# A mixer block and an attention block on one core: HGRN operands built earlier, S5 outputs asked for every six gate units, and the split-off gate units recounted

## The reference

```python
h = rms_norm(x, mix_norm)
(u_a, q_b, f_b, i_b, og_b, cx_c, v_c, o_c, ig_c, fg_c, gates) = split(h @ w_in)
y_a = s5_mixer(u_a, ...)       # complex diagonal state space, 32 groups x 64 states
y_b = hgrn2_mixer(q_b, f_b, i_b, og_b, ...)   # gated linear attention, 6 heads of 128
y_c = mlstm_mixer(cx_c, v_c, o_c, ig_c, fg_c, ...)
merged = (sigmoid(g_a) * (y_a @ wb_a) + sigmoid(g_b) * (y_b @ wb_b) + sigmoid(g_c) * (y_c @ wb_c))
x = x + merged @ w_out
x = x + conv_ffn(rms_norm(x, ffn_norm), ...)
```

## Time and profile before

| | |
|---|---|
| median of three runs | 3015.6 us |
| the profiled execution, its time | 3018.68 us |
| its span in the profile | 3016.9 us |
| PE busy | 2962.8 us (98%) |
| DVE busy | 2051.3 us (68%) |
| ACT busy | 1311.4 us (43%) |
| mean granted clock of TensorE | 0.994 |

### The profile page before, as it was taken

One profiled execution on the slowest core, in us unless ns is written; L12 is line 12 of the kernel. 1 busy time (PEld: TensorE's weight loads), 2 busy tenths in 40 slices (PEclk: granted clock), 3 DMA queues, 4 the chain that ended last, 5 costly groups with the idle time before them and its releaser, 6 DMA issues.

```text
span 3016.9 us, 47095 instructions
## 1 busy us (share of the span) xinstructions
PE 2962.8 (98%) x18616; PEld 2640.7 (88%) x18616; DVE 2051.3 (68%) x2624; ACT 1311.4 (43%) x1418; POOL 70.3 (2%) x72
## 2 busy tenths in 40 slices
PE   8999999889999999999999999999999999999999
PEld 8898898889988888888888888886998888888888
DVE  6674787866778888885557776636667666666444
ACT  5354424334444444444444344425444444444333
POOL 0000000000001000000000000000000000000000
PEclk9999999999999999999999999999999999999999
DMA  6553334445555555555555554531455555555555
GB/s 227 182 188 131 119 112 141 140 134 202 183 193 195 195 193 191 190 184 184 187 188 200 194 182 167 182 136 56 168 181 195 191 190 191 194 194 179 193 194 186
DMA packets 87359, 530.39 MB, mean 176 GB/s; under 512 B 9952, under 2 KB 10336, under 8 KB 41184
## 3 DMA queue, kind: packets, MB, share of 16 engines
q1 hardware_dynamic: 87264, 529.07, 50.4%
HBM read 526.94 MB, written 2.10 MB: 175 GB/s over the span
## 4 chain that ended last, share of the span: by engine, by line
PE 94%; DVE 4%; ACT 1%; issue 0%; DMA 0%; SPq 0%; DVEq 0%; ACTq 0%
PE bank L576 72%; PE late L576 22%; DVE arena L1670 2%; DVE half_low L1670 1%; DVE arena L1667 0%; DVE w_low L1670 0%; ACT w_high L1186 0%; DVE arena L1972 0%; PE late L1127 0%; DMA xT<-in_xT 0%; DMA ring<-in_w_gates 0%; DVE acts_both L1670 0%; DVE arena L2087 0%; DVE arena L2088 0%; DVE arena L2030 0%
## 5 line engine op out<-in xcount | busy, mean ns | idle before, releaser
L1670 DVE TENSOR_TENSOR w_low<-ring,w_high 128x2048 fp32r<-128x2048 f32 (+1 forms) x480 | 1014.4, 2114 | 388.4 <-ACT w_high L1186 384.5
L1186 ACT ACTIVATE w_high<-ring 128x2048 fp32r<-128x2048 f32 (+1 forms) x480 | 849.5, 1771 | 649.4 <-DMA ring<-in_w_down 225.9
L576 PE MATMUL bank<-up_early,w_high 128*128 128x512 f32 x1408 | 487.8, 389 | 0.0
L576 PE MATMUL bank<-up_late,w_high 128*128 128x512 f32 x1408 | 487.4, 389 | 0.0
L576 PE MATMUL late<-acts_both,w_high 128*128 128x512 f32 x1408 | 485.8, 392 | 0.3 <-DVE w_low L1670 0.3
L576 PE MATMUL late<-acts_both,w_low 128*128 128x256 f32 x1408 | 391.7, 278 | 0.0
L576 PE MATMUL bank<-up_early,w_low 128*128 128x256 f32 x1408 | 388.7, 276 | 0.0
L576 PE MATMUL bank<-up_late,w_low 128*128 128x256 f32 x1408 | 388.6, 276 | 0.0
L576 PEld LDWEIGHTS late<-acts_both,w_high 128*128 128x128 f32 x1408 | 264.5, 188 | 58.4 <-DVE w_low L1670 0.6
L576 PEld LDWEIGHTS bank<-up_early,w_high 128*128 128x128 f32 x1408 | 264.3, 188 | 55.2
L576 PEld LDWEIGHTS bank<-up_late,w_high 128*128 128x128 f32 x1408 | 264.3, 188 | 55.1
(11 more groups left out here) (311 smaller groups left out, 5041.0 us busy)
## 6 DMA issues: line engine op xcount, KB each, us to landing
ring<-in_w_up SPq DMA_DIRECT2D x176, 1024.0 KB, 4.7
ring<-in_w_down SPq DMA_DIRECT2D x128, 704.0 KB, 4.0
ring<-in_w_in SPq DMA_DIRECT2D x66, 1024.0 KB, 4.7
ring<-in_w_mix SPq DMA_DIRECT2D x62, 1024.0 KB, 4.8
ring<-in_w_gates SPq DMA_DIRECT2D x96, 512.0 KB, 3.7
ring<-in_w_branch SPq DMA_DIRECT2D x16, 1024.0 KB, 4.8
ring<-in_w_out SPq DMA_DIRECT2D x16, 1024.0 KB, 4.7
ring<-in_w_o SPq DMA_DIRECT2D x16, 1024.0 KB, 4.7
```

The source lines that it names most:

```text
L576: return nc.tensor.matmul(o, lhsT, rhs, start=first, stop=last)
L1186: A(w_high[:, s, 0:cols], ring[:, s, 0:cols], ACT.Copy).then_inc(rounded[s], 1)
L1670: return V.tensor_tensor(o, a, b, op)
```

## The change

PE has the same instructions and only their order differs: `s5_feed(3)` comes after unit 32 instead of 33, and the four S5 outputs come after units 22, 28, 34 and 40 instead of 24, 31, 38 and 43. Units 42 to 47 instead of 44 to 47 stand behind the S5 stage. PE no longer waits for `s5_gate` ahead of the first branch products.

DVE: the memset and `meet(1)` stand ahead of the scaling of the mLSTM output, `meet(2)` moves into the first turn of the level loop (behind the scores of level 0 and ahead of that turn's unit), the unit that stood behind the scaling is gone, and one more stands behind the loop. In S5 the output matrix is made in two parts, `s5_kept(f - 1)` moves behind the sums of group f, and the seventh unit of groups 2 and 3 is gone from the loop. ACT's order changes only by `GATES_FED`.

```diff
--- before.py
+++ after.py
@@ -97,7 +97,7 @@
 HEAD_ORDER = [8, 9, 10, 0, 11, 1, 12, 2, 13, 3, 14, 4, 15, 5, 6, 7]
 IN2, GATES2, TOKENS2 = 26, 32, 8
 GATES, HALF = 48, UNIT // 2
-GATES_FED = 44
+GATES_FED = 42
 
 
 def gate_of(c):
@@ -949,11 +949,10 @@
             s5_feed(0)
             for c in range(19, GATES_FED):
                 gate()
-                if c in (21, 26, 33):
-                    s5_feed({21: 1, 26: 2, 33: 3}[c])
-                if c in (24, 31, 38):
-                    s5_output({24: 0, 31: 1, 38: 2}[c])
-            s5_output(3)
+                if c in (21, 26, 32):
+                    s5_feed({21: 1, 26: 2, 32: 3}[c])
+                if c in (22, 28, 34, 40):
+                    s5_output({22: 0, 28: 1, 34: 2, 40: 3}[c])
             for c in range(GATES_FED, GATES):
                 gate()
             pe.wait_ge(s5_gelu, 1)
@@ -976,7 +975,6 @@
                     for o, lo, hi in ((bank[s][:, 1], 4, 10), (bank[RING + s][:, 0], 10, 16), (bank[s][:, 0], 0, 4)):
                         if first:
                             pe.wait_ge(y_lowered, 3 if lo == 0 else 2)
-                            pe.wait_ge(s5_gate, 1)
                         for k in range(lo, hi):
                             last = mm3(o, s, k, *y[k], k == lo, k == hi - 1)
                     return last
@@ -1978,28 +1976,6 @@
             last.then_inc(ml_h, 1)
             lower_gate()
 
-            for h in range(HG):
-                last = (V.tensor_scalar(HF[:, h], HF[:, h], lb[:, 1, h:h + 1], lb[:, 0, h:h + 1], M, ADD))
-            link(last)
-            V.tensor_scalar(HK, HF, -1.0, 1.0, M, ADD).then_inc(hg_x, 1)
-            V.memset(PD, 0.0)
-            row_factors()
-            lower_gate()
-            dve.wait_ge(norm_spread, casts[0])
-            for h in range(ML):
-                for k, p0, p1, _ in PIECES[h]:
-                    c = VAT["ml_norm"] + k
-                    last = stt(HH[p0:p1, k], HH[p0:p1, k], vec[p0:p1, c:c + 1], factor(h)[p0:p1])
-            link(last)
-            tt(MT[:, O0:O0 + 6], HH, MT[:, O0:O0 + 6]).then_inc(norm_done, 1)
-            dve.wait_ge(norm_done, 2)
-
-
-            lower_gate()
-            link(V.memset(HPR, 1.0))
-            dve.wait_ge(hg_x, 1)
-            dve.wait_ge(hmask_landed, 16)
-
             def halves(ap, B):
                 return ap.rearrange("p k t -> p (k t)").rearrange("p (n two b) -> p n two b", two=2, b=B)
 
@@ -2017,8 +1993,28 @@
                     link(tt(pr[:, :, 0], pr[:, :, 0], pf[:, :, 1, B - 1:B].broadcast_to(n)))
                     link(tt(pf[:, :, 1], pf[:, :, 1], pf[:, :, 0, B - 1:B].broadcast_to(n)))
 
+            for h in range(HG):
+                last = (V.tensor_scalar(HF[:, h], HF[:, h], lb[:, 1, h:h + 1], lb[:, 0, h:h + 1], M, ADD))
+            link(last)
+            V.tensor_scalar(HK, HF, -1.0, 1.0, M, ADD).then_inc(hg_x, 1)
+            V.memset(PD, 0.0)
+            row_factors()
+            lower_gate()
+            link(V.memset(HPR, 1.0))
+            dve.wait_ge(hg_x, 1)
             meet(1)
-            meet(2)
+            dve.wait_ge(norm_spread, casts[0])
+            for h in range(ML):
+                for k, p0, p1, _ in PIECES[h]:
+                    c = VAT["ml_norm"] + k
+                    last = stt(HH[p0:p1, k], HH[p0:p1, k], vec[p0:p1, c:c + 1], factor(h)[p0:p1])
+            link(last)
+            tt(MT[:, O0:O0 + 6], HH, MT[:, O0:O0 + 6]).then_inc(norm_done, 1)
+            dve.wait_ge(norm_done, 2)
+
+
+            dve.wait_ge(hmask_landed, 16)
+
             for lvl in range(9):
                 dve.wait_ge(hg_scored, lvl + 1)
                 if lvl == 8:
@@ -2030,10 +2026,11 @@
                         last = V.copy_predicated(PD[:, 2 * j:2 * j + 2].rearrange("p k (b c) -> p (k b) c", c=P), m,
                                                  bank_row[4 + j].rearrange("p (k c) -> p k c", c=P))
                     last.then_inc(hg_taken, 1)
-                if 1 <= lvl <= 6:
+                if lvl <= 6:
                     meet(lvl + 2)
                 if lvl < 8:
                     lower_gate()
+            lower_gate()
             lower_gate()
             row_factors()
             lower_gate()
@@ -2047,15 +2044,17 @@
 
             lower_gate()
 
-            def s5_output_matrix():
+            def s5_output_matrix(part):
                 re, im = (x.rearrange("p (n o) -> p n o", o=1).broadcast_to([P, S5_STATES, S5_ROWS]) for x in (cr, ci))
-                dve.wait_ge(s5_c_landed, 16)
-                link(tt(c_new, c_re, re))
-                link(tt(c_tmp, c_im, im))
-                link(tt(c_new, c_new, c_tmp, SUB))
-                link(tt(c_tmp, c_re, im))
-                link(tt(c_im, c_im, re))
-                tt(c_im, c_im, c_tmp, ADD).then_inc(s5_c_made, 1)
+                if part == 0:
+                    dve.wait_ge(s5_c_landed, 16)
+                    link(tt(c_new, c_re, re))
+                    link(tt(c_tmp, c_im, im))
+                    link(tt(c_new, c_new, c_tmp, SUB))
+                else:
+                    link(tt(c_tmp, c_re, im))
+                    link(tt(c_im, c_im, re))
+                    tt(c_im, c_im, c_tmp, ADD).then_inc(s5_c_made, 1)
 
             def s5_kept(f):
                 dve.wait_ge(s5_out, f + 1)
@@ -2069,7 +2068,7 @@
                     lower_gate()
                     s5_turn(f, 1)
                     lower_gate()
-                    s5_kept(f - 1)
+                    dve.wait_ge(s5_out, f)
                 dve.wait_ge(s5_fed, f + 1)
                 tt(tmp_r, turn_s, late[:, :, 0])
                 tt(SR, turn_c, late[:, :, 0])
@@ -2080,7 +2079,9 @@
                 link(tt(SR, SR, tmp_i, ADD))
                 link(tt(SI, SI, tmp_r, SUB))
                 if f == 0:
-                    s5_output_matrix()
+                    s5_output_matrix(0)
+                else:
+                    s5_kept(f - 1)
                 lower_gate()
                 for n in range(4):
                     m = mag[:, 4 * f + n:4 * f + n + 1].broadcast_to([P, T])
@@ -2092,13 +2093,14 @@
                 link(tt(SI, turn_s, tmp_r))
                 link(tt(tmp_r, turn_s, tmp_i))
                 tt(tmp_i, turn_c, tmp_i).then_inc(s5_states, 1)
+                dve.wait_ge(s5_states, f + 1)
+                if f == 0:
+                    s5_output_matrix(1)
                 lower_gate()
-                dve.wait_ge(s5_states, f + 1)
-                if f > 1:
-                    lower_gate()
-            s5_kept(S5_TILES - 1)
             for c in range(GATES_FED, GATES):
                 lower_gate()
+                if c == GATES_FED + 1:
+                    s5_kept(S5_TILES - 1)
             for m, at in enumerate((Q0, O0)):
                 dve.wait_ge(y_rounded, m + 1)
                 tt(y_low[:, at:at + 6], MT[:, at:at + 6], y_high[:, 6 * m:6 * m + 6].bitcast(F32), SUB)
```

## The result

The changed kernel takes 3059.0 us (median of four runs, 3058.7 to 3060.1) against 3014.9 us for four runs of the kernel before (3009.6 to 3016.3): a ratio of 1.015, with a 95% interval of 1.0133 to 1.0168. It is slower by 44 us; the forecast was 50. The profiled execution took 3058.77 us, its span is 3057.0 us, and the mean granted clock fell from 0.994 to 0.989.

What follows compares the result with a forecast made beforehand. The chain of waits, on PE for 94% of the span, was taken as the bound. Levels 69.6, their head +0.4, S5 -20 and the end 0 sum to +50 us: forecast 3065.6 us, range 3042 to 3092.

Steps and rivals of the forecast that it cites:

- The missing unit: HGRN levels: DVE loses its one-unit lead, PE stands 7.1 us a turn; with the clock price 69.6 us in all.
- The price of the clock: HGRN levels: after each stall PE resumes at the lower clock, +2.4 us for each of units 8 to 13.
- The rival in which the low clock never leaves: HGRN levels: 1.2 GHz holds through all turns, +41 us, so 3107; chance 0.10 for throughout or most of it.
- The head of the levels: Level 0 waits 5.3 us longer for `norm_done` at a clock cost, level 1's wait goes: net +0.4 us.
- S5: Unit 19 to the GLU: outputs at every sixth unit avoid long waits, winning 20 of 30.8 us lost.
- the 3.9 us: S5 stage: PE stands 3.9 us at the first output, waiting for the output matrix.
- The handing over: S5 stage: about 1 us lost between DVE and PE in each of three groups.
- The end: First branch products start 1.7 us earlier without `s5_gate`, but a later wait grows: 0 in the sum.

Runs made afterwards that it cites:

- the run with filled stalls: The changed kernel with 48 more matmuls, whose result nothing reads, on PE between the scores of levels 0 to 6 and the unit: 3043.6 us.
- the HGRN edits alone: The changed kernel with the S5 part of the diff and `GATES_FED` undone: 3079.5 us, ratio 1.0226.
- the run with `s5_gate` back: The kernel before plus S5 edits and `meet(2)` moved into the level loop, with PE's wait for `s5_gate` put back: 2983.4 us, ratio 0.9919.

## Why the prediction was right

**The missing unit.** The step held in place, sign and number: eight stalls, six at 6.94 to 7.04 us (forecast 6.9 of waiting, and with the 0.2 by which a unit used to overlap the 24 matmuls 7.1), then 4.97 and 3.23. Moving that one unit back took away the whole loss of 65 us.

**The price of the clock** is the term that was mis-sized. I took +2.4 us for each of units 8 to 13 from the one stall of 6.91 us before. Measured is 432.87 - 425.36 = 7.51 us from start to sigmoid instead of 6.04, so +1.5; the run with filled stalls gives 1.4 by another way. After a stall in the old S5 stage the low clock lay over 5.64 us of the resumed work; in units 8 to 13 it lay over 3.3 to 3.5. Six turns with 0.9 less are 5.4 us, which is the difference between the 70.0 us forecast for the levels and the 64.8 measured. Units 14 and 15 were as forecast, at +2.3 and +1.5. How far it was missed depends on the execution: with the HGRN edits alone, behind the same waits, unit 8 paid +2.3 us, as forecast, and the price fell from turn to turn to +1.5 at unit 13. The section of the Trainium skill that the prediction cites, "HAM oscillation — how this bites in real kernels" on the page "TensorE: Matmul & The Clock Gate", tells of a fall to the lower clock in each turn of such a loop. The trace agrees: 0.79 over the levels, 0.50 to 0.51 at the start of each of units 8 to 13. The rival in which the low clock never leaves fell: the full clock came back within every unit (1.00 from 394.90 on in unit 8).

**The head of the levels.** A wait of 5.32 us for `norm_done` and 5.49 us for the 24 matmuls in place of 4.83 and 5.46. The net of +0.4 holds; with the unit ahead the stage even shows -0.6.

**S5.** -21.1 us against a forecast of 20, and 193.4 us against 194. I counted the loss before as 30.8 us; 9.7 are left of it, where I forecast 11. The first output waits for the output matrix as I said, but the 3.9 us were only in part standing:

```profile
572.29 4.80 PE L576 MATMUL bank<-arena 128*32 128x256 f32 x32 [2.25 <-DVE arena L1668]
```

PE waited 2.25 us, and the 32 matmuls took 4.80 us instead of 3.30. The unit and the output together took 13.0 us, against 9.2 for the later outputs, so 3.8 in all. The handing over cost less than I named: the five waits for `half_low` in this stage are 3.5 us in all, the longest 0.99.

**The end.** 0, as forecast: PE waited 1.75 us for `s5_gate` and 0.69 for `y_low` before, and waits 2.69 for `y_low` alone now, and from the first GLU matmul to the first `u_high` matmul it is 13.99 us before and after.

**Sum.** 64.8 - 21.1 = 43.7 against 70.0 - 20.

## What to carry to other kernels

When several engines run orders written by hand, count for each consumer how many pieces the producer has made ahead of the first point where the producer itself waits for the consumer. A loop that makes one and takes one in each turn keeps that lead for ever, or its absence; here one unit ahead of a loop instead of behind it was worth 8.7 us in each of six turns (17.1 against 8.43), while the two moves of work around it together were worth nothing. And an edit that is right in one stage (S5, -21 us) can hide behind one that is wrong in the next: the stages have to be read apart. The S5 edits with `meet(2)` in the loop and the unit ahead of it, which the experiments point to, run at 2983 to 2985 us, 0.7 to 0.8% under the kernel before.

## What the runs showed of the hardware that was not expected

The same stall has no fixed price in clock. After a wait of 1.91 us at the same place (2.9 us of matmuls behind a wait of 1.11) the unit took 7.5 us in one execution (clock 0.77) and 6.0 in another (clock 1.00). After a wait of 2.2 us for the output matrix the 32 matmuls took 4.80 us in the changed kernel and 3.27 in the run with `s5_gate` back. After waits of about 7 us the low clock covered 5.64 us of the work that followed in the old S5 stage, and 3.3 to 3.5 in units 8 to 13 of the changed kernel, whose turns were 17.1 us long throughout. With the HGRN edits alone and the same waits, unit 8 took 8.37 us from start to sigmoid, the following ones 7.99, 7.77, 7.63 and 7.57, and unit 13 took 7.52, so the turns shrank from 17.6 to 17.1 us. What sets the share is not shown.

The first down projection, which no edit touches, took 246.7 us in the profiled executions of before, after and of the HGRN edits alone, and 240.0 in all others. The windows of after and of the filled stalls, and the group of its wide matmuls in each:

```profile
1404.20:1651.00 246.80, 246.47 (x1411) 215.56 (x1410) 138.91 (x145) 108.62 (x112) 0.00 (x0) 1.00 0.57 191
```

```profile
L576 PE MATMUL late<-acts_both,w_high 128*128 128x512 f32 x704 | 246.4, 395 | 0.3 <-DVE w_low L1668 0.3
```

```profile
1396.30:1636.30 240.00, 239.67 (x1411) 211.69 (x1410) 138.98 (x145) 108.28 (x111) 0.00 (x0) 1.00 0.59 196
```

```profile
L576 PE MATMUL late<-acts_both,w_high 128*128 128x512 f32 x703 | 239.3, 389 | 0.3 <-DVE w_low L1671 0.3
```

The granted clock is 1.00 in both, PE has no gap of note in either, and a matmul takes 395 ns in one and 389 in the other, spread evenly over the stage (145 matmuls in 25 us against 149). The cause is open. Steps of this size may be why the kernel before has runs at 3007 and at 3016 us, which no trace here shows, and they are why the stage was compared and not only the whole.
